# Packing the last two levels of a triangular inverse over all heads of a hybrid decoder block

## What is computed

```python
lower = jnp.where(tri_strict, jnp.einsum('bhnid,bhnjd->bhnij', kbc, kc) * decay, 0.0)
t_mat = lax.linalg.triangular_solve(eye + lower, jnp.broadcast_to(eye, lower.shape),
                                    left_side=True, lower=True, unit_diagonal=True)
u = jnp.einsum('bhnij,bhnje->bhnie', t_mat, vbc)
w = jnp.einsum('bhnij,bhnjd->bhnid', t_mat, kbc * jnp.exp(gc)[..., None])
```

## Time and profile before

| | us |
|---|---|
| median of 3 runs (354.47 to 354.71) | 354.5 |
| the profiled execution | 354.45 |
| its span, first to last instruction | 352.6 |
| PE busy in the span | 343.9 |
| DVE busy | 267.6 |
| ACT busy | 221.8 |
| POOL busy | 59.7 |

### The profile page before, as it was taken

The page is one execution under the profiler, slowest core; times in us unless marked ns, Lnnn a source line. Parts: engine busy times, 40 slices in busy tenths (PEclk is TensorE's granted clock), DMA queues, the critical chain, the costliest instruction groups (busy, mean ns, idle before and its releaser), DMA issues.

```text
span 352.6 us, 7455 instructions
## 1 busy us (share of the span) xinstructions
PE 343.9 (98%) x2755; PEld 331.2 (94%) x2755; DVE 267.6 (76%) x560; ACT 221.8 (63%) x499; POOL 59.7 (17%) x113
## 2 busy tenths in 40 slices
PE   6999999999999999999999999999999999999993
PEld 4889998999999999999999999999999999999882
DVE  3869797498996868978789797887967557588644
ACT  5877895445456667686866867677667655444421
POOL 1534435500033000300203011030200201000011
PEclk9999999999999999999999999999999999999999
DMA  8856947996799565646565565655564556776703
GB/s 261 245 159 196 312 129 203 233 286 156 210 245 235 139 179 128 165 129 157 143 154 146 130 170 130 172 131 146 144 162 138 170 163 184 200 241 190 250 38 119
DMA packets 100305, 62.48 MB, mean 177 GB/s; under 512 B 4676, under 2 KB 95214, under 8 KB 100270
## 3 DMA queue, kind: packets, MB, share of 16 engines
q1 hardware_dynamic: 98014, 58.59, 61.1%
q0 software_dynamic: 1072, 3.04, 2.7%
q10 hardware_dynamic: 1184, 0.39, 0.5%
HBM read 60.41 MB, written 1.59 MB: 176 GB/s over the span
## 4 chain that ended last, share of the span: by engine, by line
PE 96%; DMA 1%; ACT 1%; POOL 0%; DVE 0%; DVEq 0%; issue 0%; SPq 0%; POOLq 0%; ACTq 0%
PE banks L1331 68%; PE banks L1349 6%; PE banks L1544 6%; DMA xin<-in_x_dram 1%; PE banks L1429 1%; PE banks L1406 1%; PE banks L1446 1%; PE banks L1435 1%; PE banks L1316 1%; PE banks L1248 1%; PE banks L1273 1%; PE banks L1496 1%; PE banks L1491 1%; PE banks L1467 1%; PE banks L1471 1%; PE banks L1463 1%
## 5 line engine op out<-in xcount | busy, mean ns | idle before, releaser
L888 DVE TENSOR_TENSOR w_lo<-raw,w_hi 128x1024 fp32r<-128x1024 f32 x102 | 124.0, 1218 | 44.4 <-ACT w_hi L637 44.0
L637 ACT CAST w_hi<-raw 128x1024 fp32r<-128x1024 f32 x103 | 107.5, 1047 | 9.5 <-PE banks L1544 5.5
L1331 PE MATMUL banks<-h_hi,w_hi 128*128 128x256 f32 x568 | 81.2, 285 | 0.0
L1331 PE MATMUL banks<-h_lo,w_hi 128*128 128x256 f32 x568 | 76.5, 277 | 0.0
L1331 PE MATMUL banks<-h_hi,w_lo 128*128 128x256 f32 x568 | 76.4, 277 | 0.0
L1331 PEld LDWEIGHTS banks<-h_hi,w_hi 128*128 128x128 f32 x568 | 70.9, 189 | 0.3
L1331 PEld LDWEIGHTS banks<-h_hi,w_lo 128*128 128x128 f32 x568 | 69.9, 188 | 0.0
L1331 PEld LDWEIGHTS banks<-h_lo,w_hi 128*128 128x128 f32 x568 | 69.8, 188 | 0.0
L959 DVE SCALAR_TENSOR_TENSOR acc<-banks,vec,acc 128x255 f32<-128x255 f32 (+2 forms) x72 | 34.5, 480 | 4.3 <-ACT acc L759 2.0
L587 POOL TENSOR_TENSOR so<-so,rnq 128x2 f32<-128x2 f32 x8 | 2.6, 331 | 162.8 <-ACT junk L826 162.8
L759 ACT ACTIVATE acc<-banks,vec 128x256 f32<-128x256 f32 x16 | 7.6, 475 | 18.6 <-PE banks L1331 18.6
(11 more groups left out here) (244 smaller groups left out, 543.8 us busy)
## 6 DMA issues: line engine op xcount, KB each, us to landing
raw<-in_w_in_dram SPq DMA_DIRECT2D x80, 512.0 KB, 4.1
raw<-in_w_branch_dram SPq DMA_DIRECT2D x16, 512.0 KB, 3.7
raw<-in_w_out_dram SPq DMA_DIRECT2D x8, 512.0 KB, 3.3
xin<-in_x_dram SPq DMA_DIRECT2D x2, 512.0 KB, 3.7
th_E<-g_rows POOLq DMA_DIRECT2D x2, 512.0 KB, 7.9
bias<-bias_rows POOLq DMA_DIRECT2D x1, 1024.0 KB, 8.9
raw<-in_x_dram SPq DMA_DIRECT2D x2, 512.0 KB, 5.0
out_dram<-xin SPq DMA_DIRECT2D x4, 256.0 KB, 2.0
```

The lines of the kernel that those rows point to most:

```text
L637: nc.scalar.copy(w_hi[:, t % SLOTS, :], raw[:, t % SLOTS, :]).then_inc(s_hi, 1)
L888: v.tensor_tensor(w_lo[:, t % SLOTS, cols], raw[:, t % SLOTS, cols], w_hi[:, t % SLOTS, cols].bitcast(F32), ALU.subtract).then_inc(s_lo, 1)
L1331: last = mm(ps, w, r, start=part == 0 and k == 0, stop=part == 2 and k == KT - 1)
```

## The change

`stage_u` and `compact` go. A new `inverse(S)` on PE, DVE and ACT makes both levels for all heads together. First level: two slots, L1X = 96 and L1D = 99, each with 8 products (one a head) of 64 rows out and 64 columns; the operands hold both pairs and both chunks packed along the partitions, with zeros around, `s1_all` (the corners), `m1_all` (inverses of the even blocks 0 and 2) and `m2_all` (those of the odd blocks, turned by DVE as one 128x512 transpose). Second level: per half of the heads one slot for X (102, 120) and one for D (105, 123), each 4 products of 128x128. ACT now takes half of the copies. U of all heads lies in `la_all`'s place and is zeroed by POOL.

POOL gets new work ahead of the store (zeroing `junk`, one copy of all corners into `lac`, four loads from SBUF to SBUF into `s1_all`, zeroing `U_all`), between store and reload (zeroing 1024 and 512 columns of `sub`), and then first loads the even blocks into `m1_all` (four DMAs, 32 KB each) and behind them the four of `T_all` as before. SP loads the odd blocks (four DMAs, 32 KB each) between weight tiles 35 and 36.

```diff
-U0, W0, UW_STRIDE = 99, 114, 18
+W0, W_STRIDE = 114, 18
+L1X, L1D = 96, 99
+L2X, L2D = (102, 120), (105, 123)
...
-        lac = sb("lac", [P, 2, 2, P])
+        lac = sb("lac", [P, HEADS, P])
...
-        u2, xl, oo, on = [two(0), two(256)], two(512), two(768), two(1024)
+        oo, on = two(768), two(1024)
...
+        U_all = la_all
+        bottom, turned = sub[:, 512:1024], sub[:, 1536:2048]
+        s1_all, m1_all, m2_t, m2_all = (packed(a, HEADS) for a in (junk[:], sub[:, 0:512], bottom, turned))
+        xs_all, xl = packed(sub[:, 2048:2560], HEADS), packed(sub[:, 0:512], 4)
...
+            def odd_blocks():
+                sp.wait_ge(s_T_out, 32)
+                sp.wait_ge(s_y_zero, 4)
+                for b in range(2):
+                    for c in range(NC):
+                        lane = HALF * b + BLK * c
+                        sp.dma_start(m2_t[lane:lane + BLK, :, BLK * c:BLK * c + BLK],
+                                     t_blocks[c::NC, 2 * b + 1].rearrange("a r n -> r a n")).then_inc(s_m2_in, 16)
             for h in range(HEADS):
                 for t in range(PER_HEAD):
                     n = HEAD0 + PER_HEAD * h + t
+                    if (h, t) == (1, 2):
+                        odd_blocks()
                     load(n, n, w_tile(HEAD_COLS[t] + P * h))
...
+            pool.wait_ge(s_ksq, 2 * HEADS)
+            pool.memset(junk[:], 0.0).then_inc(s_y_zero, 1)
+            pool.tensor_copy(lac[:].rearrange("p h (c x) -> p (h c) x", c=NC),
+                             la_all[:, :, :, HALF:].rearrange("p h c x -> p (h c) x")).then_inc(s_lac, 1)
+            pool.wait_ge(s_y_zero, 1)
+            for b in range(2):
+                for c in range(NC):
+                    lane = HALF * b + BLK * c
+                    pool.dma_start(s1_all[lane:lane + BLK, :, BLK * b:BLK * b + BLK],
+                                   la_all[HALF * b:HALF * b + BLK, :, c, HALF * b + BLK:HALF * b + HALF]
+                                   ).then_inc(s_l1_in, 16)
+            pool.wait_ge(s_lac, 1)
+            pool.wait_ge(s_l1_in, 64)
+            pool.memset(U_all.rearrange("p h c n -> p (h c n)"), 0.0).then_inc(s_y_zero, 1)
             pool.wait_ge(s_sub, 2 * STEPS)
             for a in range(2):
                 pool.dma_start(bass.AP(t_blocks.tensor, BLK * a, [[BLK * BLK, HALF], [2 * BLK, BLK // 2], [1, BLK]]),
                                t0[HALF * a:HALF * a + HALF]).then_inc(s_T_out, 16)
+            pool.memset(sub[:, 0:1024], 0.0).then_inc(s_y_zero, 1)
+            pool.memset(sub[:, 2048:2560], 0.0).then_inc(s_y_zero, 1)
+            pool.wait_ge(s_y_zero, 4)
             pool.wait_ge(s_T_out, 32)
+            for b in range(2):
+                for c in range(NC):
+                    lane = HALF * b + BLK * c
+                    pool.dma_start(m1_all[lane:lane + BLK, :, BLK * c:BLK * c + BLK],
+                                   t_blocks[c::NC, 2 * b].rearrange("a r n -> r a n")).then_inc(s_l1_in, 16)
             for b in range(NBLK):
...
-            def compact(g):
...
@@ scalar @@
+            def inverse(S):
+                if S == L1X + 1:
+                    sa.wait_ge(s_inv_x, 1)
+                    found = bD[BLK:HALF, :].rearrange("p (h c n) -> p h c n", h=HEADS, c=NC)
+                    for c in range(NC):
+                        lane = HALF + BLK * c
+                        nc.scalar.copy(xs_all[lane:lane + BLK, :, BLK:HALF], found[:, :, c, :]).then_inc(s_inv_c, 1)
+                elif S == L1D + 1:
+                    sa.wait_ge(s_inv_d, 1)
+                    found = bD[BLK:HALF, :].rearrange("p (h c n) -> p (h c) n", h=HEADS, c=NC)
+                    nc.scalar.copy(U_all[HALF:HALF + BLK, :, :, HALF + BLK:].rearrange("p h c n -> p (h c) n"),
+                                   found).then_inc(s_inv_u, 1)
+                for half in range(2):
+                    found = bD[HALF:, :].rearrange("p (h c n) -> p h c n", h=4, c=NC)[:, :, 1, :]
+                    if S == L2X[half] + 1:
+                        sa.wait_ge(s_inv_x, half + 2)
+                        nc.scalar.copy(xl[HALF:, :, HALF:], found).then_inc(s_inv_c, 1)
+                    elif S == L2D[half] + 1:
+                        sa.wait_ge(s_inv_d, half + 2)
+                        nc.scalar.copy(U_all[0:HALF, 4 * half:4 * half + 4, 1, HALF:], found).then_inc(s_inv_u, 1)
...
@@ vector @@
-            def stage_u(g, s):
...
+            def inverse(S):
+                def diagonal(blocks):
+                    for i in blocks:
+                        part = slice(BLK * i, BLK * i + BLK)
+                        v.transpose(U_all[part, :, :, part].rearrange("p h c n -> p (h c) n"),
+                                    T_all[part, :, :, part].rearrange("p h c n -> p (h c) n")).then_inc(s_inv_t, 1)
+                if S == L1X:
+                    ve.wait_ge(s_m2_in, 64)
+                    v.transpose(turned, bottom).then_inc(s_inv_t, 1)
+                elif S == L1X + 1:
+                    ve.wait_ge(s_inv_x, 1)
+                    found = bD[0:BLK, :].rearrange("p (h c n) -> p h c n", h=HEADS, c=NC)
                     for c in range(NC):
-                        v.transpose(T_all[BLK:2 * BLK, g, c, 0:BLK], U[0:BLK, c, BLK:2 * BLK]).then_inc(s_u12, 1)
-                elif s == 10:
-                    ve.wait_ge(s_x_p, 2 * g + 2)
-                    for c in range(NC):
-                        v.tensor_copy(xl[HALF:, 1, HALF * c:HALF * c + HALF],
-                                      bD[HALF * c:HALF * c + HALF, 2 * P + HALF * c:2 * P + HALF * c + HALF]).then_inc(s_x, 1)
-                elif s == 13:
-                    ve.wait_ge(s_d_p, 2 * g + 2)
-                    for c in range(NC):
-                        v.tensor_copy(U[0:HALF, c, HALF:],
-                                      bD[HALF * c:HALF * c + HALF, 3 * P + HALF * c:3 * P + HALF * c + HALF]).then_inc(s_u, 1)
+                        v.tensor_copy(xs_all[BLK * c:BLK * c + BLK, :, 0:BLK], found[:, :, c, :]).then_inc(s_inv_c, 1)
+                elif S == L1D + 1:
+                    ve.wait_ge(s_inv_d, 1)
+                    corner = U_all[0:BLK, :, :, BLK:HALF].rearrange("p h c n -> p (h c) n")
+                    v.tensor_copy(corner, bD[0:BLK, :].rearrange("p (h c n) -> p (h c) n", h=HEADS, c=NC)).then_inc(s_inv_u, 1)
+                    ve.wait_ge(s_inv_u, 2)
+                    ve.wait_ge(s_T_in, 16 * NBLK)
+                    v.transpose(T_all[BLK:HALF, :, :, 0:BLK].rearrange("p h c n -> p (h c) n"), corner).then_inc(s_inv_t, 1)
+                elif S == L1D + 3:
+                    diagonal((2, 3))
+                elif S == L2D[0] + 2:
+                    diagonal((0, 1))
+                for half in range(2):
+                    found = bD[0:HALF, :].rearrange("p (h c n) -> p h c n", h=4, c=NC)[:, :, 0, :]
+                    if S == L2X[half] + 1:
+                        ve.wait_ge(s_inv_x, half + 2)
+                        v.tensor_copy(xl[HALF:, :, 0:HALF], found).then_inc(s_inv_c, 1)
+                    elif S == L2D[half] + 1:
+                        ve.wait_ge(s_inv_d, half + 2)
+                        v.tensor_copy(U_all[0:HALF, 4 * half:4 * half + 4, 0, HALF:], found).then_inc(s_inv_u, 1)
...
@@ tensor @@
-            def stage_u(g, s):
...
+            def inverse(S):
+                if S == L1X:
+                    pe.wait_ge(s_l1_in, 128)
+                    pe.wait_ge(s_k0, HEADS)
+                    for h in range(HEADS):
+                        last = mm(bD[0:HALF, HALF * h:HALF * h + HALF], s1_all[:, h, :], m1_all[:, h, :], start=True, stop=True)
+                    last.then_inc(s_inv_x, 1)
+                elif S == L1D:
+                    pe.wait_ge(s_inv_c, 4)
+                    pe.wait_ge(s_inv_t, 1)
+                    for h in range(HEADS):
+                        last = mm(bD[0:HALF, HALF * h:HALF * h + HALF], xs_all[:, h, :], m2_all[:, h, :], start=True, stop=True)
+                    last.then_inc(s_inv_d, 1)
+                for half in range(2):
+                    if S == L2X[half]:
+                        pe.wait_ge(s_lac, 1)
+                        if half:
+                            pe.wait_ge(s_inv_u, 4)
+                        else:
+                            pe.wait_ge(s_inv_u, 2)
+                            pe.wait_ge(s_inv_t, 2)
+                        for i in range(4):
+                            last = mm(bD[:, P * i:P * i + P], lac[:, 4 * half + i, :], T_all[:, 4 * half + i, :, 0:HALF], start=True, stop=True)
+                        last.then_inc(s_inv_x, 1)
+                    elif S == L2D[half]:
+                        pe.wait_ge(s_inv_c, 2 * half + 6)
+                        pe.wait_ge(s_inv_t, 4)
+                        for i in range(4):
+                            last = mm(bD[:, P * i:P * i + P], xl[:, i, :], U_all[:, 4 * half + i, :, HALF:], start=True, stop=True)
+                        last.then_inc(s_inv_d, 1)
```

(29 more changed lines are left out.)

60 lines of the change are left out of this document (removed).

## The result

The kernel with the change takes **361.14 us** (360.37 to 362.76, 6 runs), the kernel before 354.74 us beside it (6 runs): ratio 1.0182, 95% interval 1.0167 to 1.0198. The forecast was 356.5 with a range of 353.8 to 358.6. The sign was right and the size was not: 6.4 us slower instead of 2.0, outside the range. The profiled execution is the quickest of the six, 360.37 us with a span of 358.2.

What follows compares the result with a forecast made beforehand. The prediction took PE, busy 98% of the span, to bound the kernel: 354.45 us, less 0.9 of PE work, plus 3.0 of wait for the even blocks, gave 356.5 us, range 353.8 to 358.6.

Steps and rivals of the forecast that it cites:

- What bounds the kernel, and which wait decides: PE, busy 98%, sets the time; the one new wait is at L1X in slot 96, for the even-block loads.
- Rivals 1 and 2: 1: even loads land in time, 353.6 us, chance 0.15; 2: wait only 0.3 to 1.6 us, 353.8 to 355.2, chance 0.12.
- PE work: Products on PE: 7.1 us removed, 3.5 and 2.7 added, so 0.9 us less, between 0 and 1.9.
- The first wait: Slot 96, L1X: PE ready at 107.7, last even block lands at 110.7; wait 3.0 us, ends 1.1 and 5.8.
- rival 3: Small loads land as late as large ones, fourth at 113.5; wait 5.8 us, 359.3 us; chance 0.07.
- Rival 4: A chain of waits, or PE returning at 1.2 GHz, the latter 1 to 1.8 us more, 357.5 to 358.3; chance 0.11.
- Rival 5: POOL's copy holds up DVE in 71 to 80 us: 0.8 us more, 357.3; chance 0.07, inside the forecast's.
- SyncE: SP's four odd-block issues send load 36 out at about 106.3, 0.4 us late but hidden by 1.7 us; cost 0.
- Later waits: At L1D, L2X and L2D (slots 99, 102, 105) the data is ready in time; 0 paid, 1.0 us kept for the high end.

Runs made afterwards that it cites:

- the versions without a wait: Changed kernel with L1X at slot 102: 354.73 us; that with ACT making the lac copy and earlier diagonal turns: 354.69; the last with L1X at slot 100: 354.56.
- the old kernel with the wait: Kernel before, with PE also waiting in slot 96 for all four reloads of T_all: 360.60 us, ratio 1.0180.
- the filled version: Changed kernel with 34 extra, overwritten 128x256 products on PE ahead of the wait for the even blocks: 358.51 us, ratio 1.0120.
- the half-filled version: Changed kernel with 17 extra, overwritten products on PE ahead of the even-block wait, leaving a wait of 1.8 us: 359.88 us, ratio 1.0152.
- one tile later: Changed kernel with L1X at slot 99, L1D 102, L2X 105, L2D 108 and a separate scratch for ACT's squares: 355.08 us, ratio 1.0013.
- two tiles later: Changed kernel with L1X at slot 102, L1D 105, L2X 108, L2D 111 and a separate scratch for ACT's squares: 354.73 us, ratio 1.0003.
- that kernel's runs: Changed kernel with POOL's copy into lac and zeroing of U_all moved behind the store of the solved blocks: 358.96 us, ratio 1.0119.
- even blocks through SP: Changed kernel with the four even-block loads on SP's queue ahead of the odd ones, instead of POOL's: 360.97 us, ratio 1.0187.
- odd blocks later: Changed kernel with SP's odd-block loads one weight tile later, behind load 36: 360.31 us, ratio 1.0168.
- copy by ACT: Changed kernel with ACT instead of POOL copying the corners into lac, in slot 58; L1X stays at 96: 359.60 us, ratio 1.0146.

## Why the prediction went wrong, step by step

- **What bounds the kernel, and which wait decides: right.** PE work and PE waits set the end; there is one new wait, at the first L1X product, ended by a load from t_blocks. Rivals 1 and 2 are out: in no profile of the order as changed did the last even block come within 1.6 us of the end of slot 95.
- **PE work: right in size, by two errors.** The first-level products take 0.134 us each against the 0.17 I chose between 0.11 and 0.22; the middle of two ends was a poor choice, the low end was nearer. A head period fell by 0.82 us against 0.9. Eight heads give 6.6, less 16 x 0.134 = 2.1 and the second-level groups, 4 x 0.89 = 3.6: 0.9, as forecast. But in the versions without a wait the stretch where the groups stand is 0.65 us longer than this sum, the first-level edges of 0.1 us each being part of it, and it begins 0.3 us late. These versions measure what is left: 0.0 us, within 0.6. The forecast's gain of 0.9 did not arrive.
- **The first wait: the term was 1.2 us too small.** The landing came at 112.25 rather than 110.7, and PE was ready at 108.05 rather than 107.7. The landing has three pieces. POOL began its first load at 105.15, where the forecast had 104.45; the store had gone out 0.7 us late, and between its landing and the first load lie 0.56 us, as in every profile with the change whose chain shows it (0.56 or 0.57), where the old kernel with the wait has 0.28. I can't say why it is longer here. The issue of three took 1.76, as against the 1.95 I had. And the last load took 5.34 us instead of 4.3. The last is the misread step. I took the landing of the data from what had gone through the queue by 108 us. But the four landings of 32 KB took 3.6, 3.7, 3.5 and 5.3 us, and the four of 64 KB in the old kernel with its wait 4.5, 4.2, 4.0 and 5.3. Half the bytes brought the first three in somewhat sooner and the last, on which the wait hangs, no sooner. That was the mechanism of rival 3, with less than its price.
- **The clock: the step that failed.** The sum put it at nothing. Rival 4 said that an idle PE of 3 us could come back at 1.2 GHz, priced it at 1 to 1.8 us from the first products of the kernel and gave it 0.11. It should have been in the sum, which would then have been 357.5 to 358.3. The row that spoke against it was an idle time of 1.1 us ahead of 8.0 us, a third as long as the wait I forecast. The measured price is 1.8 us in the profile of after, and 2.6 us by the medians of after and the filled version, above the upper end of mine. That the price came as near as it did is partly luck. It was taken from a row whose granted clock the profile of before gives as 1.00, so that row doesn't show the lower clock at all (window below). The Trainium skill (TensorE: Matmul & The Clock Gate, section "HAM oscillation — how this bites in real kernels") has waits for DMA as what drops the clock. The traces agree: a wait of 4.2 us did it in after, and one of 1.8 us in the half-filled version.

```profile
2.00:4.00 2.00, 2.00 (x6) 1.55 (x6) 0.00 (x0) 0.04 (x2) 0.00 (x0) 1.00 0.91 358
```

- **Rival 5, POOL holds DVE: mechanism right, effect not shown.** The hold is 1.6 to 1.8 us, more than the copy's length. I had it at 1.7 less 0.9 us of idle. The store was issued at 97.44 with the hold (96.73 in before), at 96.71 with it and the odd loads later, at 97.55 without it. Over all profiles with the change it goes out at 96.71 to 97.67 with the hold (seven) and at 96.51 to 97.55 without it (four). So it doesn't follow the hold in a way that can be seen, and what moves it by about 1 us stays open. Nor is an earlier store always an earlier landing: gone out at 96.71 it landed at 104.29, gone out at 97.08 (one tile later) at 104.06. The Trainium skill (SBUF — State Buffer, section "SBUF: two separate sides") gives the shared port pair to whoever starts first, for the whole instruction, and counts a DVE instruction with two inputs only against a GpSimd one that reads. The traces agree that a two-input DVE instruction loses beside a reading copy and that a zeroing doesn't do it. They don't bear out who wins: by the profile the DVE instruction had started first both times (70.82 against 71.50, 97.27 against 98.08) and still lost, and the hold exceeded the copy by 0.5 to 0.7 us. In before a w_lo that had started first (106.87) took its usual 1.23 us, and the POOL copy at 107.06 paid, with 1.18 us. Starts on POOL are rough in the profile, so the order is not certain.
- **SyncE: cost 0, right, by a larger margin used.** The four issues took 3.0 us and not 1.9 (0.45, 0.45 and 1.5 us among them), load 36 went out at 107.65 and not 106.3. As PE was late, nobody noticed.
- **Later waits: 0, right.** None at L1D, L2X, L2D or later.

The sum of the errors: 1.2 in the wait, 1.8 (profile) to 2.6 (medians) for the clock, 0.9 of gain that did not arrive. That is 3.9 to 4.7, against 360.4 - 356.5 = 3.9 for the profiled run and 361.1 - 356.5 = 4.6 for the median.

## What to carry to other kernels

Where PE is busy to 98% and a change makes it wait for a load once, add the clock to the wait: here waits of 1.8 to 4.3 us, where the clock fell, cost 1.6 to 2.6 us more behind them, and a rival with a known price and a wait of its size in the forecast belongs in the sum. Put the first use of reloaded data where its slowest landing is over (here two tiles later undid the whole loss in the median, though single runs suggest that the landing can still be late), and don't count on the last of several smaller loads landing sooner. And check what remains of a saving in products against where it is first paid: new groups of small products cost more than their own length.

## What the runs showed of the hardware beyond that

- **The clock isn't decided by the length of the wait alone.** 0.7 us held it; 1.8 us dropped it; 2.1 us held it in one profiled run, and the mean clocks of that kernel's runs (0.997 and 0.996, 0.991 and 0.988) say that it was dropped in two of four. After waits of 4.0 to 4.3 us it was down in all four profiles that have one (after, even blocks through SP, odd blocks later, copy by ACT: 0.50 to 0.66 in 112 to 114 us).
- **The fall need not come in the wait.** It came 1.8 us before PE started again (copy by ACT), as it started (after), and 0.9 us after it was back at full work (the old kernel with the wait). The pieces behind the wait are 2.6, 1.8 and 1.6 us there; the clock was low from 110.7 to 117.5 us in the first and from 112.3 to 115.7 in the second.
- **A 128*64 product by 64 columns takes 0.134 us**, not the 0.11 that half of the 0.22 us of a full product would be, and the lines around the group lose 0.1 to 0.2 us.
- **The last of four 32 KB loads lands no quicker than the last of four 64 KB ones** in this stretch, DMA share 1.2: 5.3 us in both, the three ahead of it 3.5 to 3.7 against 4.0 to 4.5; and one value of 7.1 in one execution of before shows how far a single profile's landing can be from the next.
- **A reading copy on POOL stops a two-input DVE instruction for longer than it runs**: 1.05 us of copy, 1.6 us of hold; 1.12 us, 1.8 us.
